# A two-block fp32 model on one core: row broadcasts and square sums from rounded parts, gate activations in pairs, and a reordered delta-rule stage

## The chip, the cores and the metric

The kernel runs on one core of one Trainium2 chip. The metric is the device time of one execution in microseconds, as the median of several executions. All data is fp32 with 512 tokens, and the model's width D is 1024. An activation lies feature-major in SBUF, as 8 tiles of 128 features by 512 tokens.

## What is computed

The reference is a chain of two blocks. Cut to its order and to the parts that the change touches:

```
h = x + 0.5*ffn1(norm(x))
proj = norm(h) @ w_in                       # hybrid mixer ("mixer1")
z, xbc, dt, q, k, v = split(proj)
xs, B, C = split(silu(causal_conv(xbc)))
dt = softplus(dt + dt_bias); a = -exp(a_log)
y = ssd_chunked(xs, dt, a, B, C, d_skip)    # 16 heads of 64
y = norm(y * silu(z))
h = h + concat(y, chunked_rel_attention(q, k, v)) @ w_out
h = norm(h + 0.5*ffn2(norm(h)))
# second block, layer 0: gated delta rule ("mixer2"), 8 heads of 128
q, k, v = split(silu(causal_conv(norm(h) @ w_qkv)))
q, k = l2_norm(q)*128**-.5, l2_norm(k)
beta = sigmoid(b_in); g = -exp(a_log)*softplus(a_in + dt_bias)
G = cumsum(g) in chunks of 64
decay[r,s] = exp(G[r] - G[s]), s <= r
solve (I + strict(beta * k k^T * decay)) [u, w] = [beta v, beta exp(G) k]
o = recurrence over chunks; o = norm(o) * silu(gate)
h = h + o @ w_out; h = h + ffn(norm(h)); h = h + embedding part
# layer 1: stick-breaking attention ("mixer3"), 8 heads of 128
k = norm_per_head(norm(h) @ w_k); q = norm_per_head(norm(h) @ w_q)*128**-.5
```

Then come the attention of mixer3, its FFN and its embedding part.

## The kernel before

Weights stream through one pipeline of 405 units, each 128 partitions by 1024. A unit comes by DMA into one of two `raw` slots. ACT rounds it to `w_hi` (L403, type fp32r), POOL computes `w_lo` = raw - w_hi (L2470), and there are four slots of these. The activations are split in the same way into `x_hi` and `x_lo` (or `mid_hi` and `mid_lo`). PE forms each fp32 product from three fp32r matmuls: hi by hi, lo by hi, hi by lo. A unit for 128 output features is then 24 matmuls of 128 rows by 512 columns. Each engine has its own program, written out by hand in Python functions (`pe_mixer1`, `act_mixer1`, `dve_mixer1` and so on); semaphores join them, and the order on each engine is the order of the code.

**Mixer1.** The cumulative sums of the 16 heads' decays lie in `cs_row`, 16 partitions by 512. For each head x, `broadcast(x)` (L719) spreads row x over 128 partitions into a PSUM bank: an fp32 matmul whose weights are column x of the identity, repeated. DVE subtracts the column form (`exponents`, L1106), ACT takes exponentials (`decays`, L969 and L972), DVE multiplies by C B^T (`weights`, L1119), and PE multiplies by the scaled inputs (`y_pair(m)`, L736 and L741, two heads each). A loop of eight rounds m does this for the heads 2m+2 and 2m+3 and for y_pair(m). Between these, PE works at the 8 units of z (`gate_fill`, L646 to L648), as filler. z of round m+1 goes from PSUM through DVE (`z_out`, L1123) and ACT (`z_silu`, L977); Silu is in another of ACT's function tables than Exp, so ACT loads a table before it and one after it. `gate` (L1131) multiplies y by silu(z), ACT squares it (L992), and `round_at` does the L403 rounding of one weight unit.

**Mixer2.** Units of q, k and v come first; each passes `conv_tile` on DVE (L1731, L1735, L1737 three times) and `conv_silu` on ACT (L1624). Log decays and betas lie in `g_row`, 40 partitions by 512 (rows 0 to 7 and 32 to 39). `decay_broadcast` (L1372) and `beta_broadcast` (L1377) spread one row each, as in mixer1. The heads go in four pairs p. In each, the triangular solve doubles an inverse over levels n: PE L1471, ACT `em` (L1656), PE L1502, DVE L1881 and the transpose L1884. A pair's setup, its four broadcasts too, is done in the levels of the pair before it, and that of pair 0 among the units. `FILLS[p]` names the three filler units that PE does during pair p: units of the output gate (L1324 to L1326, from `x_hi`) and of the output projection (L1335 to L1337, from `mid_hi` and `mid_lo`, which pair p-1 has to have finished). L1452 is the sum of a pair's output norm.

**Mixer3.** Sixteen units give k and q. ACT squares each 128x512 tile, and PE adds over the partitions with a matrix of ones (`square_sum`, L2084, fp32).

## Time and profile before

| | before |
|---|---|
| time, median of 3 runs | 2642.24 us (2640.12 to 2644.57) |
| profiled execution, its own time | 2639.76 us |
| its span | 2638.0 us |
| mean granted TensorE clock | 0.995 |
| busy PE / DVE / ACT / POOL | 98% / 39% / 41% / 40% of the span |
| HBM | 84 GB/s over the span |

The span runs from the first to the last instruction; 1.76 us of the execution's own time lie around it. The profile counts an engine busy while an instruction is in it. Matmuls are pipelined and overlap in the records, so the distance between two starts tells what one costs, not its duration. One fp32 matmul is recorded as two. In a timeline the columns are the start, the time in us, engine, line, operation, output<-inputs and the count; in brackets stands the idle time of the engine just before, with what ended it. A row of windows gives the stretch, its length, the busy time (and instructions) of PE, PEld (weight loads), DVE, ACT and POOL, the granted TensorE clock (1.00 is full speed), the DMA share and GB/s.

### The profile page before, as it was taken

What the parts mean: (1) busy time and instruction counts of PE and PEld (TensorE: products, weight loads), DVE (VectorE), ACT (ScalarE), POOL (GpSimd) and SP (SyncE); (2) the same over time, 40 slices, a digit from 0 to 9 for tenths busy, and PEclk for the clock granted to TensorE, in tenths of its full rate; (3) what the DMA queues carried; (4) which work ended last, traced back from release to release, by engine and by line L of the source; (5) the groups of instructions that cost most, each with busy time, mean ns of one, the idle gap of its engine ahead of it and who ended that gap; (6) DMA issues with size and microseconds to landing.
All of it is one profiled execution on the core that took longest, in us unless ns stands there. A gap on an engine that the chain in (4) does not pass through costs nothing.

```text
span 2638.0 us, 32543 instructions
## 1 busy us (share of the span) xinstructions
PE 2593.3 (98%) x12090; PEld 2100.3 (80%) x12090; DVE 1041.8 (39%) x1477; ACT 1089.7 (41%) x1567; POOL 1060.8 (40%) x466
## 2 busy tenths in 40 slices
PE   9999999999999999999999999999999999999999
PEld 7888887776888888777878878888877777888887
DVE  4212223966522122787456542122372344211224
ACT  5222233678432223565445542223355464222233
POOL 4444443222444444335334344444443222444444
PEclk9999999999999999999999999999999999999999
DMA  4232332111232222222000122322322112222233
GB/s 158 95 101 93 102 125 77 62 56 57 88 103 98 94 96 95 80 80 80 17 25 25 33 96 95 104 89 95 103 89 79 56 48 80 96 96 96 95 103 113
DMA packets 61719, 222.68 MB, mean 84 GB/s; under 512 B 6704, under 2 KB 6832, under 8 KB 61488
## 3 DMA queue, kind: packets, MB, share of 16 engines
q1 hardware_dynamic: 60928, 218.07, 25.0%
q10 hardware_dynamic: 688, 3.15, 0.3%
q8 instruction: 75, 1.23, 0.2%
q14 instruction: 28, 0.23, 0.0%
HBM read 219.10 MB, written 2.10 MB: 84 GB/s over the span
## 4 chain that ended last, share of the span: by engine, by line
PE 91%; DVE 6%; issue 2%; ACT 1%; DMA 0%; SPq 0%; DVEq 0%; ACTq 0%
PE ps L358 13%; PE ps L360 13%; PE ps L359 13%; PE ps L385 6%; PE ps L384 6%; PE ps L383 6%; PE ps L646 2%; PE ps L647 2%; PE ps L648 2%; PE ps L1471 1%; PE ps L1502 1%; PE ps L2187 1%; PE ps L1412 1%; PE ps L1414 1%; PE ps L1413 1%
## 5 line engine op out<-in xcount | busy, mean ns | idle before, releaser
L2470 POOL TENSOR_TENSOR w_lo<-raw,w_hi 128x1024 fp32r<-128x1024 f32 x405 | 981.9, 2426 | 1471.5 <-ACT w_hi L403 1471.5
L403 ACT ACTIVATE w_hi<-raw 128x1024 fp32r<-128x1024 f32 x405 | 424.9, 1050 | 468.2 <-PE ps L385 294.2
L358 PE MATMUL ps<-x_hi,w_hi 128*128 128x512 f32 x1536 | 600.7, 391 | 5.1 <-DVE x_lo L436 5.1
L359 PE MATMUL ps<-x_lo,w_hi 128*128 128x512 f32 x1536 | 597.7, 389 | 0.0
L360 PE MATMUL ps<-x_hi,w_lo 128*128 128x512 f32 x1536 | 597.6, 389 | 0.0
L358 PEld LDWEIGHTS ps<-x_hi,w_hi 128*128 128x128 f32 x1536 | 288.3, 188 | 69.9 <-DVE x_lo L436 6.7
L359 PEld LDWEIGHTS ps<-x_lo,w_hi 128*128 128x128 f32 x1536 | 288.3, 188 | 60.8 <-issue 1.4
L360 PEld LDWEIGHTS ps<-x_hi,w_lo 128*128 128x128 f32 x1536 | 288.3, 188 | 60.0
L383 PE MATMUL ps<-mid_hi,w_hi 128*128 128x512 f32 x736 | 286.3, 389 | 0.0
L384 PE MATMUL ps<-mid_lo,w_hi 128*128 128x512 f32 x736 | 286.3, 389 | 0.0
L385 PE MATMUL ps<-mid_hi,w_lo 128*128 128x512 f32 x736 | 286.3, 389 | 0.0
L530 DVE TENSOR_TENSOR ff_up<-ps,rstd 128x512 f32<-128x512 f32 x88 | 60.8, 691 | 398.5 <-PE ps L360 398.5
L499 ACT ACTIVATE mid_hi<-ff_up 128x512 f32 (+1 forms) x88 | 55.6, 632 | 384.6 <-DVE ff_up L533 384.6
L554 DVE SCALAR_TENSOR_TENSOR h<-ps,h 128x512 f32<-128x512 f32 x64 | 43.8, 690 | 392.3 <-PE ps L385 392.3
L384 PEld LDWEIGHTS ps<-mid_lo,w_hi 128*128 128x128 f32 x736 | 138.2, 188 | 28.8
L383 PEld LDWEIGHTS ps<-mid_hi,w_hi 128*128 128x128 f32 x736 | 138.2, 188 | 28.7
L385 PEld LDWEIGHTS ps<-mid_hi,w_lo 128*128 128x128 f32 x736 | 138.2, 188 | 28.5
L496 ACT ACTIVATE ff_gate<-ff_gate 128x512 f32<-128x512 f32 x88 | 55.6, 632 | 247.8 <-DVE ff_gate L528 247.7
L528 DVE TENSOR_TENSOR ff_gate<-ps,rstd 128x512 f32<-128x512 f32 x88 | 60.8, 691 | 221.2 <-PE ps L360 200.8
L1957 POOL TENSOR_TENSOR ao<-at,const 128x512 f32<-128x512 f32 x48 | 66.5, 1404 | 98.9 <-PE ps L1471 81.2
L535 DVE TENSOR_TENSOR mid_lo<-ff_up,mid_hi 128x512 f32 x88 | 66.9, 761 | 80.1 <-ACT mid_hi L499 80.1
L646 PE MATMUL ps<-x_hi,w_hi 128*128 128x512 f32 x232 | 94.0, 405 | 0.3 <-DVE x_lo L436 0.3
...
## 6 DMA issues: line engine op xcount, KB each, us to landing
...
```

The costliest lines, as they stand in the source:

```text
L358: nc.tensor.matmul(out, hi, x_hi[:, k, :], start=(k == 0), stop=False)
L359: nc.tensor.matmul(out, hi, x_lo[:, k, :], start=False, stop=False)
L360: last = nc.tensor.matmul(out, lo, x_hi[:, k, :], start=False, stop=(k == DK - 1))
L383: nc.tensor.matmul(out, hi, r_hi, start=(k == 0), stop=False)
L384: nc.tensor.matmul(out, hi, r_lo, start=False, stop=False)
L385: last = nc.tensor.matmul(out, lo, r_hi, start=False, stop=(k == tiles - 1))
L403: nc.scalar.activation(w_hi[:, n % W_SLOTS, :], raw[:, n % RAW_SLOTS, :], ACT.Copy).then_inc(s_whi, 1)
L528: nc.vector.tensor_tensor(ff_gate[:, pair, :], ps[:, 4 * g + j % 4, :], rstd[:, :], ALU.mult).then_inc(s_free, 1)
L535: nc.vector.tensor_tensor(tile_at(mid_lo, done), ff_up[:, pair, :], tile_at(mid_hi, done).bitcast(F32), ALU.subtract).then_inc(s_mlo, 1)
L646: nc.tensor.matmul(out, hi, x_hi[:, k, :], start=(k == 0), stop=False)
L1957: nc.gpsimd.tensor_tensor(gw["ao"][j][:, :, :], gw["at"][j][:, :, :], merge, ALU.mult).then_inc(s_gao, 1)
L2470: nc.gpsimd.tensor_tensor(w_lo[:, n % W_SLOTS, :], raw[:, n % RAW_SLOTS, :], w_hi[:, n % W_SLOTS, :].bitcast(F32), ALU.subtract).then_inc( ...
```

## The change

1. Mixer1's 16 broadcasts. A tile `cs_parts` holds the rounded rows in partitions 0 to 15 and the rests in 64 to 79; `sel` is built once, with ones at x and at 64+x. The broadcast becomes one fp32r matmul over 80 rows. DVE builds `cs_parts` with a memset, a copy and a subtraction (semaphore `s_csp`).
2. Mixer2's 16 broadcasts, in the same way over 104 rows (`g_parts`; one ACT copy and two DVE subtractions, `s_gpt`).
3. Mixer1's z. Silu is applied to tiles 0 and 1 before the loop, and then to two tiles at once in rounds 2, 4 and 6. DVE's `z_out` runs two tiles ahead. PE takes 16 instead of 8 of the gate filler's pieces before the loop, so that the loop's last two rounds have output units as filler.
4. Mixer2's last convolution (unit 23 of q, k, v) moves on DVE and ACT from before level 0 of pair 0 to behind the updates of level 0.
5. `FILLS[1]`: gate 3, out(0,0), gate 4 becomes gate 3, gate 4, out(0,0).
6. Mixer3's 16 square sums. DVE squares, ACT copies a rounded part (in place of squaring), DVE subtracts, and PE adds both parts with two fp32r matmuls.

```
-FILLS = ((("gate", 0), ("gate", 1), ("gate", 2)), (("gate", 3), ("out", 0, 0), ("gate", 4)),
+FILLS = ((("gate", 0), ("gate", 1), ("gate", 2)), (("gate", 3), ("gate", 4), ("out", 0, 0)),
...
             def broadcast(x):
                 if x == 0:
+                    pe.wait_ge(s_sel, 1)
+                    pe.wait_ge(s_csp, 3)
...
-                nc.tensor.matmul(ps[:, SPREAD[x % 2], :], ident[0:SSD_HEADS, x:x + 1].to_broadcast([SSD_HEADS, P]), cs_row[:, :],
+                nc.tensor.matmul(ps[:, SPREAD[x % 2], :], sel[0:64 + SSD_HEADS, x:x + 1].to_broadcast([64 + SSD_HEADS, P]), cs_parts[:, :],
...
-            take(gates, 8)
+            take(gates, 16)
...
+                if m < 6:
                     take(gates, 4)
+                else:
+                    out_unit(n_t, 0, 0, (0, 1) if m == 6 else (2, 3))
+                if m < 7:
                     broadcast(2 * m + 3)
-                else:
-                    out_unit(n_t, 0, 0, (0, 1))
                 y_pair(m)
-                if m < 7:
+                if m < 6:
                     take(gates, 4)
             assert next(gates, None) is None
-            out_unit(n_t, 0, 0, (2, 3))
...
             z_silu(0)
+            z_silu(1)
             for m in range(8):
                 if m < 7:
                     decays(2 * m + 2)
+                if m in (2, 4, 6):
+                    z_silu(m)
+                    z_silu(m + 1)
+                if m < 7:
                     decays(2 * m + 3)
...
-                if m < 7:
-                    z_silu(m + 1)
...
+                    if x == 6:
+                        nc.vector.memset(cs_parts[:, :].bitcast(F32), 0.0).then_inc(s_csp, 1)
+                        dve.wait_ge(s_csp, 1)
+                        nc.vector.tensor_copy(cs_parts[0:SSD_HEADS, :], cs_row[:, :]).then_inc(s_csp, 1)
+                        dve.wait_ge(s_csp, 2)
+                        nc.vector.tensor_tensor(cs_parts[64:64 + SSD_HEADS, :], cs_row[:, :], cs_parts[0:SSD_HEADS, :].bitcast(F32), ALU.subtract).then_inc(s_csp, 1)
...
                 if p:
                     pe.wait_ge(s_gqk, x - 1)
-                nc.tensor.matmul(ps[:, SETUP[j], :], ident[0:40, x:x + 1].to_broadcast([40, P]), g_row[:, :], start=True, stop=True).then_inc(s_gbc, 1)
+                elif j == 0:
+                    pe.wait_ge(s_gpt, 3)
+                nc.tensor.matmul(ps[:, SETUP[j], :], sel[0:104, x:x + 1].to_broadcast([104, P]), g_parts[:, :], start=True, stop=True).then_inc(s_gbc, 1)
...
+                if u == 9:
+                    act.wait_ge(s_ga2, 2)
+                    nc.scalar.activation(g_parts[0:40, :], g_row[:, :], ACT.Copy).then_inc(s_gpt, 1)
...
                 if u == 24:
+                    conv_tile(22, 23)
...
+                    if p == 0 and n == 0:
+                        conv_tile(23, 24)
...
-                nc.tensor.matmul(ps[:, 4 + c % 4, :], ones, n_sq3[:, c % 4, :], start=True, stop=True).then_inc(s_nsum, 1)
+                nc.tensor.matmul(ps[:, 4 + c % 4, :], ones_r[:, :], n_hi3[:, c % 4, :], start=True, stop=False)
+                nc.tensor.matmul(ps[:, 4 + c % 4, :], ones_r[:, :], n_lo3[:, c % 3, :], start=False, stop=True).then_inc(s_nsum, 1)
...
-                nc.scalar.activation(n_sq3[:, c % 4, :], src, ACT.Square).then_inc(s_nsq, 1)
+                nc.scalar.activation(n_hi3[:, c % 4, :], n_sq3[:, c % 3, :], ACT.Copy).then_inc(s_nhi, 1)
...
+                if u >= 3:
+                    dve.wait_ge(s_nsum, SUMS + u - 2)
+                dve.wait_ge(s_free, b0 + u + 5)
+                nc.vector.tensor_tensor(n_sq3[:, u % 3, :], dest, dest, ALU.mult).then_inc(s_n32, 1)
+                if u:
+                    square_lo(u - 1)
```

ACT in the middle of mixer1's loop, before. It is one round, from one square (`sq`) to the next; `zs` is z, `decay` the exponentials.
```order
L992 ACTIVATE sq<-zs 128x512
L403 ACTIVATE w_hi<-raw 128x1024
L977 ACT_TABLE_LOAD
L977 ACTIVATE zs<-zs 128x512
L969 ACT_TABLE_LOAD
L969 ACTIVATE decay<-ps,bias_c 128x128 x6
L972 ACTIVATE decay<-decay,bias_c 128x128 x4
L969 ACTIVATE decay<-ps,bias_c 128x128 x6
L972 ACTIVATE decay<-decay,bias_c 128x128 x4
L992 ACTIVATE sq<-zs 128x512
```

The same engine after, from the square of round 1 to that of round 2:
```order
L1009 ACTIVATE sq<-zs 128x512
L409 ACTIVATE w_hi<-raw 128x1024
L981 ACTIVATE decay<-ps,bias_c 128x128 x6
L984 ACTIVATE decay<-decay,bias_c 128x128 x4
L989 ACT_TABLE_LOAD
L989 ACTIVATE zs<-zs 128x512 x2
L981 ACT_TABLE_LOAD
L981 ACTIVATE decay<-ps,bias_c 128x128 x6
L984 ACTIVATE decay<-decay,bias_c 128x128 x4
L1009 ACTIVATE sq<-zs 128x512
```

The gate's activation with its table load and the load back to Exp stood in each round, ahead of both groups of exponentials. Now two tiles stand behind one load, between the two groups of round 2, and round 1 has no load. Over the program ACT's table loads go from 106 to 99.

DVE around level 0 of mixer2's first pair, before: `tm<-tt` is the transpose of the first inverse, `cv` the last convolution, L1881 the update of level 0.
```order
L1770 STREAM_TRANSPOSE tm_117<-tt_115 128x512
L1785 TENSOR_TENSOR g_exp<-g_exp,cols_97 128x32
L1731 TENSOR_TENSOR ps<-ps,rstd 128x512
L1735 TENSOR_SCALAR cv_102<-ps,vec 128x512
L1737 SCALAR_TENSOR_TENSOR cv_102<-ps,vec,cv_102 128x511
L1737 SCALAR_TENSOR_TENSOR cv_102<-ps,vec,cv_102 128x510
L1737 SCALAR_TENSOR_TENSOR cv_102<-ps,vec,cv_102 128x509
L1881 TENSOR_TENSOR tt_114<-tt_114,ps 128x512
L1884 STREAM_TRANSPOSE tm_116<-tt_114 128x512
L1881 TENSOR_TENSOR tt_115<-tt_115,ps 128x512
L1884 STREAM_TRANSPOSE tm_117<-tt_115 128x512
L1865 TENSOR_TENSOR qkt_122<-ps,dm_126 128x512
```

After:
```order
L1805 STREAM_TRANSPOSE tm_120<-tt_118 128x512
L1821 TENSOR_TENSOR g_exp<-g_exp,cols_100 128x32
L1921 TENSOR_TENSOR tt_117<-tt_117,ps 128x512
L1924 STREAM_TRANSPOSE tm_119<-tt_117 128x512
L1921 TENSOR_TENSOR tt_118<-tt_118,ps 128x512
L1924 STREAM_TRANSPOSE tm_120<-tt_118 128x512
L1766 TENSOR_TENSOR ps<-ps,rstd 128x512
L1770 TENSOR_SCALAR cv_105<-ps,vec 128x512
L1772 SCALAR_TENSOR_TENSOR cv_105<-ps,vec,cv_105 128x511
L1772 SCALAR_TENSOR_TENSOR cv_105<-ps,vec,cv_105 128x510
L1772 SCALAR_TENSOR_TENSOR cv_105<-ps,vec,cv_105 128x509
L1905 TENSOR_TENSOR qkt_125<-ps,dm_129 128x512
```

The convolution's five operations went from ahead of the level's updates to behind them.

PE in pair 1 of mixer2, before: `g_row,const` are the decay broadcasts, `tt,em` and `tm,ao` the products of the levels, `mid_hi` and `mid_lo` belong to the unit out(0,0).
```order
L1372 MATMUL ps<-g_row,const 128x512 x2
L1502 MATMUL ps<-tt_114,em_110 128x128 x4
L1502 MATMUL ps<-tt_115,em_111 128x128 x4
L1335 MATMUL ps<-mid_hi,w_hi 128x512
L1336 MATMUL ps<-mid_lo,w_hi 128x512
L1337 MATMUL ps<-mid_hi,w_lo 128x512
L1335 MATMUL ps<-mid_hi,w_hi 128x512
L1336 MATMUL ps<-mid_lo,w_hi 128x512
L1337 MATMUL ps<-mid_hi,w_lo 128x512
L1471 MATMUL ps<-tm_116,ao_108 128x128 x4
L1471 MATMUL ps<-tm_117,ao_109 128x128 x4
```

After, at the same rows of the order:
```order
L1396 MATMUL ps<-g_parts,sel 128x512 x2
L1526 MATMUL ps<-tt_117,em_113 128x128 x4
L1526 MATMUL ps<-tt_118,em_114 128x128 x4
L1346 MATMUL ps<-x_hi,w_hi 128x512
L1347 MATMUL ps<-x_lo,w_hi 128x512
L1348 MATMUL ps<-x_hi,w_lo 128x512
L1346 MATMUL ps<-x_hi,w_hi 128x512
L1347 MATMUL ps<-x_lo,w_hi 128x512
L1348 MATMUL ps<-x_hi,w_lo 128x512
L1495 MATMUL ps<-tm_119,ao_111 128x128 x4
L1495 MATMUL ps<-tm_120,ao_112 128x128 x4
```

The broadcasts read `g_parts` and `sel`, and the filler here is now a unit of the gate; out(0,0) comes later in the pair.

## Rows read from the trace of the kernel before

**Rows 1.** The page: busy time, and the chain that ended last, by engine.
```profile
PE 2593.3 (98%) x12090; PEld 2100.3 (80%) x12090; DVE 1041.8 (39%) x1477; ACT 1089.7 (41%) x1567; POOL 1060.8 (40%) x466
...
PE 91%; DVE 6%; issue 2%; ACT 1%; DMA 0%; SPq 0%; DVEq 0%; ACTq 0%
```

**Rows 2.** Timeline of PE: two broadcasts of mixer2's head, then 16 rounded matmuls.
```profile
1206.36 0.39 PE L1414 MATMUL ps<-x_hi,w_lo 128*128 128x512 f32 x1
1206.68 1.98 PE L1372 MATMUL ps<-g_row,const 40*128 40x512 f32 x4
...
1208.92 0.40 PE L1413 MATMUL ps<-x_lo,w_hi 128*128 128x512 f32 x1
...
1222.67 0.40 PE L1412 MATMUL ps<-x_hi,w_hi 128*128 128x512 f32 x1
...
1226.08 0.39 PE L1412 MATMUL ps<-x_hi,w_hi 128*128 128x512 f32 x1
```

**Rows 3.** Timeline of PE at one broadcast in mixer1's loop.
```profile
579.08 1.12 PE L719 MATMUL ps<-cs_row,const 16*128 16x512 f32 x2
580.13 0.44 PE L736 MATMUL ps<-decay,xdt 128*64 128x128 f32 x4
```

**Rows 4.** Timeline of PE in mixer3: two square sums, 24 rounded matmuls between them.
```profile
2012.11 1.02 PE L2084 MATMUL ps<-n_sq,const 128*128 128x512 f32 x2
...
2018.46 0.59 PE L2084 MATMUL ps<-n_sq,const 128*128 128x512 f32 x1
```

**Rows 5.** One round of mixer1's loop: busy times; timelines of DVE and ACT.
```profile
573.33:584.08 10.75, 10.75 (x62) 7.07 (x61) 7.10 (x10) 10.40 (x25) 2.38 (x1) 1.00 0.15 49
...
576.24 0.69 DVE L1106 TENSOR_TENSOR decay<-ps,cols 128x512 f32<-128x512 f32 x1 [0.80 <-PE ps L719]
...
577.51 1.48 DVE L1119 TENSOR_TENSOR decay<-decay,cb 128x1280 f32<-128x1280 f32 x1
...
574.93 1.28 ACT L977 ACT_TABLE_LOAD   x1
```

**Rows 6.** Mixer1's last round: timelines of DVE, POOL and PE.
```profile
639.88 3.36 DVE L1119 TENSOR_TENSOR decay<-decay,cb 128x1280 f32<-128x1280 f32 x1
...
639.50 2.40 POOL L2470 TENSOR_TENSOR w_lo<-raw,w_hi 128x1024 fp32r<-128x1024 f32 x1 [8.38 <-ACT w_hi L403]
...
643.30 0.44 PE L736 MATMUL ps<-decay,xdt 128*64 128x128 f32 x4 [1.34 <-DVE decay L1119]
```

**Rows 7.** Windows: the number before the DMA share is the granted clock.
```profile
643.00:647.00 4.00, 3.70 (x34) 2.79 (x35) 1.47 (x3) 0.00 (x0) 0.00 (x0) 1.00 0.33 122
1246.00:1250.00 4.00, 4.00 (x18) 3.90 (x19) 1.72 (x3) 1.24 (x2) 2.36 (x1) 0.50 0.00 0
```

**Rows 8.** Timelines of DVE and PE in mixer2's head and level 0.
```profile
1227.64 0.70 DVE L1731 TENSOR_TENSOR ps<-ps,rstd 128x512 f32<-128x512 f32 x1 [1.95 <-PE ps L1414]
...
1240.83 0.69 DVE L1731 TENSOR_TENSOR ps<-ps,rstd 128x512 f32<-128x512 f32 x1
...
1242.34 2.32 DVE L1737 SCALAR_TENSOR_TENSOR cv<-ps,vec,cv 128x511 f32<-128x511 f32 x3
...
1245.86 0.58 PE L1502 MATMUL ps<-tt,em 128*128 128x128 f32 x1 [4.11 <-ACT em L1656]
```

**Rows 9.** Timeline of PE in mixer2's pairs: norm sums (L1452) and waits.
```profile
1306.75 0.70 PE L1452 MATMUL ps<-o_sq,const 128*128 128x512 f32 x1 [0.95 <-ACT o_sq L1697]
...
1337.12 0.76 PE L1335 MATMUL ps<-mid_hi,w_hi 128*128 128x512 f32 x1 [3.83 <-DVE mid_lo L1859]
...
1377.79 0.70 PE L1452 MATMUL ps<-o_sq,const 128*128 128x512 f32 x1 [0.95 <-ACT o_sq L1697]
...
1406.29 0.35 PE L1471 MATMUL ps<-tm,ao 128*128 128x128 f32 x1 [0.55 <-DVE tm L1884]
...
1443.58 0.70 PE L1452 MATMUL ps<-o_sq,const 128*128 128x512 f32 x1 [0.95 <-ACT o_sq L1697]
...
1472.08 0.55 PE L1471 MATMUL ps<-tm,ao 128*128 128x128 f32 x1 [2.60 <-DVE tm L1884]
```

More of the change, by code:

```diff
@@ L261, in build @@
         total_c = place("total_c", M + 50 * KB + 1184, [P, NB, SSD_HEADS])
+        cs_parts = place("cs_parts", M + 14 * KB, [64 + SSD_HEADS, T], F32R)
         y_tmp = place("y_tmp", M + 16 * KB, [P, 2, T])
@@ L267, in build @@
         v2 = place("v2", M + 32 * KB, [P, 8, T])
-        g_row = place("g_row", M + 48 * KB, [40, T])
+        g_row = place("g_row", MID_HI + 38 * KB, [40, T])
+        g_parts = place("g_parts", M + 48 * KB, [104, T], F32R)
         cols2 = place("cols2", M + 50 * KB, [P, NB, 40])
@@ L592, in build @@
         s_csb = sem("cumsum_broadcast")
+        s_sel = sem("row_selectors_ready")
+        s_csp = sem("cumsum_parts_ready")
+        s_gpt = sem("gdn_row_parts_ready")
         s_dec = sem("decay_ready")
@@ L1376, in beta_broadcast @@
                 pe.wait_ge(s_gem, x + 1)
-                nc.tensor.matmul(ps[:, SETUP[j], :], ident[0:40, 32 + x:33 + x].to_broadcast([40, P]), g_row[:, :], start=True, stop=True).then_inc(s_gbb, 1)
+                nc.tensor.matmul(ps[:, SETUP[j], :], sel[0:104, 32 + x:33 + x].to_broadcast([104, P]), g_parts[:, :], start=True, stop=True).then_inc(s_gbb, 1)
             def products_of_k(p, j):
@@ L1596, in norms, with conv_silu @@
                 nc.scalar.activation(n_rs[:, :, :], n_rs[:, :, :], ACT.Exp, scale=-0.5).then_inc(s_nrs, 1)
+            def conv_silu(c):
+                act.wait_ge(s_conv, 12 + c + 1)
+                dest = qk2[:, c, :] if c < 16 else v2[:, c - 16, :]
+                nc.scalar.activation(dest, cv2[:, c % 4, :], ACT.Silu).then_inc(s_convact, 1)
             for u in range(N_QKV):
@@ L1716, in dve_mixer2 @@
             ch.step(nc.vector.memset(g_row[:, :], 0.0))
+            nc.vector.memset(g_parts[:, :].bitcast(F32), 0.0)
             dve.wait_ge(s_rfin, 1)
@@ L1812, in dve_mixer2 @@
                     nc.vector.tensor_copy(cols2[:, :, :], ps[:, 7, 0:256].rearrange("p (a c) -> p a c", a=NB)[:, :, 0:40]).then_inc(s_gcol, 1)
+                if u == 10:
+                    dve.wait_ge(s_gpt, 1)
+                    for at in (0, 32):
+                        nc.vector.tensor_tensor(g_parts[64 + at:72 + at, :], g_row[at:at + 8, :], g_parts[at:at + 8, :].bitcast(F32), ALU.subtract).then_inc(s_gpt, 1)
                 if u == 22:
```

38 lines of the change are left out of this document (26 added, 12 removed).

## The prediction

> **What bounds the kernel now.** I read the page first: PE is busy 98% of the span and holds 91% of the chain that ended last, DVE 6%; DVE, ACT and POOL are busy 39 to 41% [rows 1]. So the kernel is bound by PE nearly everywhere. Time comes from cheaper PE work, or from one of its few waits; work added to the other engines is free as long as it makes no new wait on PE. Next the PE timeline gives the price of each kind of matmul, the distance between two starts. Last I read where another engine ends PE's wait: ACT or DVE once in mixer1's last round [rows 6], at level 0 of mixer2 [rows 8], and in its pairs [rows 9]. The windows tell what such a wait costs beyond itself: after one of 4.11 us the granted clock is 0.50, which is 1.2 GHz, for the four microseconds behind it; after one of 1.34 us it stays 1.00, which is 2.4 GHz [rows 7].
>
> **The price of a broadcast.** Fifteen rounded matmuls take 1226.08 - 1222.67 = 3.41 us, so 0.227 each. Two fp32 broadcasts and two rounded matmuls take 1208.92 - 1206.36 = 2.56 us, so 2.56 - 0.454 = 2.106 for the two, 1.05 each [rows 2]. Mixer1's are the same: 1.05 from the broadcast's start to the next matmul's [rows 3]. The square sums, fp32 too, but over all 128 rows, cost less: two starts with 24 rounded matmuls between them are 6.35 us apart, less 24 x 0.227 = 5.45, leaves 0.90 [rows 4]. The new broadcast is one rounded 128x512 matmul over 80 or 104 rows. Lower bound 0.227; upper bound, if a matmul of fewer than 128 rows keeps what a K=16 or 40 one has over the full one, 1.05 - 0.90 = 0.15 more. I take 0.227, since it is nearly a full one and of the type of its neighbours. The matmul behind a broadcast also starts about 0.1 late in every second case (1206.36 to 1206.68 is 0.32, not 0.227 [rows 2]). Saving: 1.05 - 0.23 + 0.05 = 0.87 each.
>
> The Trainium skill (TensorEngine Tiling (Array Packing), Key Properties) says that a change of tiling mode drains TensorE, and gives row tiling to contractions of up to 64 rows; 80 and 104 are beyond that, so by it no drain would remain, and the difference of 1.05 to 0.90 agrees with it. By the page the sum would be the one below; if the drain stayed it would be rival A.
>
> **Mixer1's loop.** A round lasts 10.75 us, PE is busy for all of it and ACT for 10.40 [rows 5]. PE's work becomes 10.75 - 2 x 0.82 - 0.1 = 9.0. ACT could not follow at 10.40; the paired silus take away 2 x 1.28 of table loads in rounds without z [rows 5], leaving 7.8, and in a round with two z it has 10.40 + 0.69 = 11.1 (a second silu, taken as long as DVE's pass over 128x512), which the rounds around it make up for. DVE's chain is next: a broadcast lands (0.39), exponents and scaled inputs take 577.51 - 576.24 = 1.27, L1119 takes 1.48 [rows 5], plus 0.1 of hand-over: 3.25 from one broadcast to the next, against PE's 0.227 + 12 x 0.227 = 2.95. So PE waits 0.3 in a plain round. L1119 is worse where POOL works: the same operation took 3.36 beside a w_lo that started 0.38 us before it, so 1.88 more [rows 6]. In the shorter round it meets a w_lo oftener. I followed the instructions of all eight rounds forward by these durations: extra waits of 1.4, 0.7, 1.5 and 0.7 in rounds 1, 2, 4 and 6, 0.3 in each of the other three, and 3.1 in the last instead of 1.34 [rows 6], since round 6's pair (two table loads and two silus, 2 x 1.28 + 2 x 0.69 = 3.9) makes its decays late. Gain: 16 x 0.87 = 13.9, less 4.3, 0.9 and 1.8, makes **7** (5 if the waits are doubled in the rounds with POOL, 9 if POOL is never in the way). Building `cs_parts` I cost at nothing: it lies in DVE's part among units, where PE has its own 5.45 us of work per unit and DVE one conv; without that cover it costs three operations, 1.5.
>
> The Trainium skill (SBUF — State Buffer, Terms) says that VectorE and GpSimd share a port pair, held for the full instruction, and that "the loser fully blocks". The 3.36 beside 1.48 agrees. It speaks against this change, which puts more two-input work on DVE; by it alone the loop would lose what I subtract above, and mixer3 could become rival B.
>
> **Mixer2's head.** Its four broadcasts save PE 3.5, but DVE sets the pace here: it waited for PE only 1.95 [rows 8], so 1.95 counts. Then level 0. PE waited 4.11 for ACT's `em` [rows 8], which stood behind the silu of the last convolution; that convolution ran on DVE from 1240.83 to 1244.66, 3.83 us [rows 8]. Moved behind the level, it takes this wait away. But the transposes of v in level 1 still need it, and PE has only about 1 us of work beside it: a new wait of 2.9 (0 to 3.8). The clock of 0.50 in the four microseconds after [rows 7] costs 2.0; the new wait is between 1.34, without a fall, and 4.11, with one, so I count half, 1.0. Sum 1.95 + 4.11 - 2.9 + 1.0 = **4.2** (2 to 7).
>
> **Mixer2's pairs.** During pair 0: four broadcasts, 3.5, of which I count **3.0**, as some wait for ACT. During pair 1: the filler out(0,0) made PE wait 3.83 for `mid_lo`. The period from norm sum to norm sum is 1377.79 - 1306.75 = 71.04; the next, with the same kinds of work and no such wait, is 1443.58 - 1377.79 = 65.79 [rows 9]. The difference, **5.25**, is the wait and the slow clock behind it, and the reorder takes it: gate 4 needs only `x_hi` and its weights, and out(0,0) comes some 10 us later, when `mid_lo` has been written. Broadcasts in pairs 1 and 2: eight, but the four decay broadcasts come just before a wait of 0.55 for DVE's transpose at 1406.29 [rows 9], which grows by what they save; the four beta broadcasts count, 4 x 0.87 less a little: **3.3**. Pair 3's waits (2.60 at 1472.08 [rows 9]) are untouched. New waits of 2 to 3 us in all this can lower the clock once: **-1.1**, half of a 2 us drop. Mixer2 together: 4.2 + 3.0 + 5.25 + 3.3 - 1.1 = 14.65. Extra ACT and DVE work for `g_parts` is three small operations in units 9 and 10, where DVE waits for PE.
>
> **Mixer3.** A square sum costs 0.90 and becomes 2 x 0.227: 0.45 x 16 = **7.1**. A unit shortens from 6.35 to 5.9. DVE now has three 128x512 operations for each (scaling, square, rest), 3 x 0.69 = 2.1 by the nearest row [rows 5], plus a w_lo's 2.40 [rows 6] if it is in the way: 4.5 of 5.9. Covered, so 0 here; if two w_lo's block it each time, rival B.
>
> **Sum.** 7 + 14.65 + 7.1 = 28.75. From the profiled execution, 2639.76, this leads to 2611.0. The median of before lies 2.48 above that execution: 2642.24 - 28.75 = **2613.5**.
>
> **Rivals.** A: the short matmuls keep their surcharge. 32 x 0.15 = 4.8, a little of it hidden where DVE sets the pace: 4, so 2617.5. For it: both fp32 broadcasts with few rows show the surcharge [rows 2 to 4]. Against: 80 and 104 rows are most of the array. Chance 0.10. B: DVE bounds mixer3. Each unit needs DVE for 2.1 + 2 x 2.40 = 6.9 instead of PE's 5.9, 16 us over sixteen units: 2629.5. For it: every added square and rest can meet a w_lo. Against: one w_lo falls to one unit in the steady state, and 4.5 fits. Chance 0.10. C, slower than before: PE's clock falls to 1.2 GHz after the new waits of mixer1's loop and mixer2 and stays down. To take back the gain of 28.75 and 5.3 more, the margin below, needs 34 us lost, that is 68 us of PE time at half clock, about a whole loop of mixer1; the time would be 2648 or more. It decides from eight rounds' worth of low clock. Against: the clock was 1.00 after a wait of 1.34 [rows 7], and the loop's waits are mostly smaller. Chance 0.03. D: the change does nothing to the time, since PE's shorter work turns into equal waits in all three stages: 2642, chance 0.04. It needs DVE chains within 1 us of PE everywhere, against DVE's 7.10 of 10.75 in the busiest loop [rows 5]. The forecast itself: 0.73.
>
> **Range.** The forecast's terms, with their ends: mixer1 5 to 9, mixer2 9 to 18, mixer3 5 to 7.1; ends that don't all fall together give 2604 to 2622, which holds nearly all of the forecast's 0.73 and rival A, 0.8 in all. B, C and D lie outside. A difference of 0.2%, about 5.3 us, is what a measurement of this kernel can tell from no change. Faster by more: forecast, A and B, with a little less for a combination, 0.93; within it: 0.04; slower: 0.03.
>
> **What would show it.** In the profile after: a broadcast on PE takes 0.23 to the next start (0.38 would be A). Mixer1's rounds are 9.3 to 10.5, with a wait for L1119's successor of some 3 us in the last. Level 0 of pair 0 has no wait for `em`; one of about 3 us stands before the v transposes. The wait for `mid_lo` in pair 1 is gone, and the period is near 64. In mixer3 the units are 5.9 apart and PE waits for nothing; a wait for the squares or for a bank (B) would make the prediction too low. Wrong, too, if the mean clock falls below 0.99.

## The result and the profile after

The changed kernel takes 2622.19 us, the median of four runs (2620.69 to 2628.02), against 2641.18 (2638.73 to 2644.57) before: a ratio of 0.9934, with a 95% interval of 0.9921 to 0.9946. Measured again beside other kernels it took 2620.37 against 2643.18, ratio 0.9915 (0.9899 to 0.9930). So it is 19 to 23 us faster. I had forecast 28.75 us less. The direction was right; the size was not, and the first median lies 0.2 us above the range; the second, 2620.37, lies inside it.

The profiled execution is the slowest of the four (2628.02, span 2626.2), so what it shows must be split into what the change did and what that execution had. The page, its rows for [rows 1]:
```profile
PE 2566.5 (98%) x12058; PEld 2097.4 (80%) x12058; DVE 1088.5 (41%) x1517; ACT 1080.9 (41%) x1561; POOL 1066.2 (41%) x466
...
PE 87%; DVE 9%; issue 2%; ACT 1%; DMA 0%; SPq 0%; DVEq 0%; ACTq 0%
```

PE is busy for 26.8 us less. The span is only 11.8 us shorter, and DVE went from 6% of the chain to 9%: the work taken off PE partly became waits for DVE.

To see where the time went I set the start of each w_lo on POOL (405 in every kernel, one for each weight unit), and of L1452 (now L1476), against the same one before. The differences by stage, in us, negative where a stage became shorter (the experiments are explained below; the last row is a second profile of the kernel before). "pair3+" is pair 3 and the rest of mixer2, "attn3" all from mixer3's attention on; nothing was changed in either:

```
                start  mixer1  head+pair0  pair1  pair2  pair3+  mixer3  attn3
forecast          0     -7.0      -7.2     -6.9   -1.6     0      -7.1     0
changed         +2.2    +0.3      -5.8     -3.7   -0.4   -2.5     -3.7   +2.0
e1_again        +2.3    -6.0      -5.4     -4.1   -1.6     0      -3.6   +0.3
e2_no_mixer1    +3.9     0        -7.6     -3.7   -0.5   -2.5     -3.7   +1.7
e3_no_sums3     +2.3    -7.7      -6.1     -4.2   -1.6     0       0     +0.3
e4_full_rows    -0.2    -7.8      -6.2     -4.1   -1.5   +0.1     -3.6   +0.3
e5_no_fills     +0.5    -3.8      -6.3     -2.4   -0.3   -1.1     -3.7   +1.9
e6_no_conv      +2.6    -6.1      -3.9     -2.6   -0.4     0      -3.8    0
e7_no_bcast2    +2.6    -7.8      -3.6     -3.7    0     -0.9     -3.7    0
e8_no_z         -0.3    -5.1      -6.2     -3.7   -0.4   -0.1     -3.8    0
e9_ahead_first  +1.8    -6.1      -6.0     -4.2   -1.6     0      -6.6   +0.2
e10_w_first     -0.4    -8.2      -5.0     -4.1   -1.6     0      -3.7   +0.2
e11_both        +3.9    -8.1      -7.3     -3.7   -0.4     0      -6.6   +1.9
e12_before      +2.0     0        +0.2     +0.1    0       0       0     -0.1
```

Of the forecast, 1.1 for slow clock stands in no column. "Start" is the lag at the fortieth unit, ahead of all that was changed. The last row says that a lag of this size needs no change: the same w_lo starts at 216.18 in the kernel before, at 218.34 in the changed one and at 218.13 in the second profile of the kernel before.

The two columns in which nothing was changed show mostly what the clock does. In pair 3 of the kernel before the granted clock is 0.74 and 0.83 over 1470 to 1478 us, and 0.61 over 1520 to 1524, behind waits of 2.60 and 2.78; in the profile of the changed kernel it is 1.00 at both places behind waits of 2.59 and 2.78, which makes the 2.5 us. It lost 2.0 again in mixer3's attention (last section). So a gain of 2.5 and a loss of 2.0 in this profile belong to no part of the change.

Mixer1 in the changed kernel. PE's timeline at two broadcasts (for [rows 3]) and at the longer waits of the rounds:
```profile
569.73 0.48 PE L730 MATMUL ps<-cs_parts,sel 80*128 80x512 f32 x1
570.05 0.40 PE L655 MATMUL ps<-x_hi,w_hi 128*128 128x512 f32 x1
572.57 0.39 PE L657 MATMUL ps<-x_hi,w_lo 128*128 128x512 f32 x1
573.05 0.49 PE L730 MATMUL ps<-cs_parts,sel 80*128 80x512 f32 x1
573.48 0.44 PE L747 MATMUL ps<-decay,xdt 128*64 128x128 f32 x4
...
583.47 0.49 PE L730 MATMUL ps<-cs_parts,sel 80*128 80x512 f32 x1 [1.22 <-DVE decay L1134]
...
624.56 0.79 PE L730 MATMUL ps<-cs_parts,sel 80*128 80x512 f32 x1 [2.32 <-DVE decay L1134]
```

The windows of the same kernel behind the last of these waits, with the granted clock ahead of the DMA share:
```profile
624.00:632.00 8.00, 7.44 (x36) 5.13 (x37) 4.63 (x6) 3.44 (x12) 0.00 (x0) 0.57 0.21 66
```

A broadcast is one matmul now; the next one starts 0.32 or 0.43 us after it, instead of 1.05. In rounds 1, 2, 4 and 5 there are waits of 1.22, 0.65 (at 593.30), 1.24 (at 613.04) and 2.32 us before the second broadcast; I had 1.4, 0.7 and 1.5 in the first three, and 0.7 in round 6 instead of one in round 5. Around the last the granted clock is 0.57 over eight microseconds, so it was at 1.2 GHz for most of them and at 2.4 for the rest. It fell a second time, to 0.79 over 640 to 648, at the last wait of the loop (3.13 at 645.78). Who holds PE up is seen on DVE:
```profile
610.37 2.61 DVE L1134 TENSOR_TENSOR decay<-decay,cb 128x1280 f32<-128x1280 f32 x1
614.19 1.48 DVE L1134 TENSOR_TENSOR decay<-decay,cb 128x1280 f32<-128x1280 f32 x1
...
620.81 3.69 DVE L1134 TENSOR_TENSOR decay<-decay,cb 128x1280 f32<-128x1280 f32 x1
```

and on POOL in the same stretch:
```profile
609.23 2.40 POOL L2527 TENSOR_TENSOR w_lo<-raw,w_hi 128x1024 fp32r<-128x1024 f32 x1 [4.43 <-ACT w_hi L409]
620.77 2.38 POOL L2527 TENSOR_TENSOR w_lo<-raw,w_hi 128x1024 fp32r<-128x1024 f32 x1 [9.14 <-ACT w_hi L409]
```

L1134, the L1119 of before, takes 1.48 where POOL is idle (614.19), 2.61 when a w_lo began 1.14 before it, and 3.69 when one began 0.04 before it. That is the blocking of [rows 6], in a place where PE waits for it. Waiting for the rest of the w_lo's 2.40 and then taking 1.48 would be 2.74 and 3.84, within 0.15 of both. The Trainium skill (SBUF — State Buffer, Terms) calls the port pair of VectorE and GpSimd exclusive for a full instruction; the three durations agree.

Mixer2 in the changed kernel, PE's timeline at the new wait for the v transposes (L1506), the waits of pair 1, and the norm sums that answer to [rows 9]:
```profile
1251.09 0.44 PE L1506 MATMUL ps<-const,v 128*128 128x128 f32 x2 [2.57 <-DVEq L1778]
...
1303.39 0.70 PE L1476 MATMUL ps<-o_sq,const 128*128 128x512 f32 x1 [0.95 <-ACT o_sq L1731]
...
1331.89 0.35 PE L1495 MATMUL ps<-tm,ao 128*128 128x128 f32 x1 [2.20 <-DVE tm L1924]
...
1361.07 0.50 PE L1357 MATMUL ps<-mid_hi,w_hi 128*128 128x512 f32 x1 [1.86 <-DVE gate L1874]
...
1370.73 0.70 PE L1476 MATMUL ps<-o_sq,const 128*128 128x512 f32 x1 [0.95 <-ACT o_sq L1731]
```

The wait of 4.11 for `em` is gone, and one of 2.57 stands at the v transposes, as forecast (2.9). The wait of 3.83 for `mid_lo` is gone too. But two others stand in pair 1: 2.20 for DVE's transpose, and 1.86 for DVE's `gate`, at the unit out(0,0) in its new place. DVE starts that `gate` only at 1360.36, straight after an inverse and its transpose (L1803 at 1358.13, L1805 at 1359.72).

Mixer3 in the changed kernel: PE's timeline from one square sum to the next:
```profile
1975.98 0.39 PE L2128 MATMUL ps<-n_hi,ones_r 128*128 128x512 f32 x1
...
1981.88 0.39 PE L2128 MATMUL ps<-n_hi,ones_r 128*128 128x512 f32 x1
...
1988.59 0.50 PE L2128 MATMUL ps<-n_hi,ones_r 128*128 128x512 f32 x1 [0.66 <-DVE n_lo L2387]
```

DVE's timeline there, with the square (L2396) and the rest (L2387):
```profile
1976.98 0.69 DVE L2396 TENSOR_TENSOR n_sq<-k 128x512 f32<-128x512 f32 x1
...
1982.87 2.85 DVE L2396 TENSOR_TENSOR n_sq<-k 128x512 f32<-128x512 f32 x1
1985.65 2.88 DVE L2387 TENSOR_TENSOR n_lo<-n_sq,n_hi 128x512 fp32r<-128x512 f32 x1
```

and POOL's:
```profile
1982.77 5.21 POOL L2527 TENSOR_TENSOR w_lo<-raw,w_hi 128x1024 fp32r<-128x1024 f32 x2 [8.73 <-ACT w_hi L409]
```

A plain unit takes 1981.88 - 1975.98 = 5.90, as forecast; the next takes 6.71, with a wait of 0.66 for the rest `n_lo`. There POOL has two w_lo's back to back, 5.21 us, and DVE's square and rest take 2.85 and 2.88 instead of 0.69.

### The profile page after: what moved, and what is told of

It is laid out like the page before. It is cut to its first block, busy times and chain, and to the rows that moved or that the text cites. A ratio compares the mean times of both kernels' runs of the same rounds, so it can differ in the third digit from the quotient of the medians.

```text
span 2626.2 us, 32527 instructions
## 1 busy us (share of the span) xinstructions
PE 2566.5 (98%) x12058; PEld 2097.4 (80%) x12058; DVE 1088.5 (41%) x1517; ACT 1080.9 (41%) x1561; POOL 1066.2 (41%) x466
## 4 chain that ended last, share of the span: by engine, by line
PE 87%; DVE 9%; issue 2%; ACT 1%; DMA 0%; SPq 0%; DVEq 0%; ACTq 0%
PE ps L364 13%; PE ps L366 13%; PE ps L365 13%; PE ps L390 6%; PE ps L391 6%; PE ps L389 6%; PE ps L655 2%; PE ps L656 2%; PE ps L657 2%; PE ps L2232 1%; PE ps L1495 1%; PE ps L1526 1%; DVE cv L1772 1%; PE ps L1436 1%; PE ps L1437 1%
## 5 line engine op out<-in xcount | busy, mean ns | idle before, releaser
L541 DVE TENSOR_TENSOR mid_lo<-ff_up,mid_hi 128x512 f32 x88 | 66.9, 760 | 80.1 <-ACT mid_hi L505 80.1
```

The costliest lines, as they stand in the source:

```text
L541: nc.vector.tensor_tensor(tile_at(mid_lo, done), ff_up[:, pair, :], tile_at(mid_hi, done).bitcast(F32), ALU.subtract).then_inc(s_mlo, 1)
```

## The experiments

All are compared with the kernel before on the same chip. The median of one and the same kernel moves by about 2 us from one measurement to the next (2641.18 to 2643.18 before, 2622.19 and 2620.37 after), so the parts are read from the traces, in the table above, and the medians only confirm them. Each stage of a variant is one profiled execution.

**e1_again** is the changed kernel once more.

> The changed kernel once more, unchanged. Theory 1 (chance falls of the clock): in the trace of the changed kernel the granted clock fell in mixer1's loop (0.57 over 624 to 632 us, 0.79 over 640 to 648), which cost about 6 us there, and again behind a wait of 2.35 us in mixer3's attention, 2 us, and the first units ran 2.2 us late; a second profile will miss at least one of these, and mixer1 will then show a gain near 6 us over before instead of a loss of 0.3. Theory 2 (the loop's new waits always bring the clock down): the second profile shows the same falls at the same places, and mixer1 gains nothing again. Time: about 2621 by the first, 2622 to 2628 by the second.

Measured: 2620.37 us, ratio 0.9915 (0.9899 to 0.9930). Mixer1 gains 6.0 in this profile and lost 0.3 in the first. The windows over the stretch in which the clock had fallen:
```profile
624.00:632.00 8.00, 7.94 (x51) 5.89 (x47) 7.64 (x9) 6.44 (x21) 3.09 (x2) 1.00 0.18 66
```

PE's timeline at the last wait of the loop:
```profile
640.74 0.44 PE L747 MATMUL ps<-decay,xdt 128*64 128x128 f32 x4 [2.04 <-DVE decay L1134]
```

Here round 5 has no such wait (0.11) and round 6 has one of 0.82, and the clock stayed at 1.00 over 624 to 632. It fell only at the last wait, to 0.79 over 640 to 648. DVE's and POOL's timelines show what made the difference in round 5, to be held against 620.81 and 620.77 above:
```profile
620.99 1.48 DVE L1134 TENSOR_TENSOR decay<-decay,cb 128x1280 f32<-128x1280 f32 x1
```

and
```profile
621.01 3.69 POOL L2527 TENSOR_TENSOR w_lo<-raw,w_hi 128x1024 fp32r<-128x1024 f32 x1 [9.19 <-ACT w_hi L409]
```

In the first profile w_lo began 0.04 us before L1134, and L1134 took 3.69; here it began 0.02 us after it, L1134 took 1.48, and it was w_lo that took 3.69 instead of 2.40. Of the two, the one that started first was not held up. Theory 1 holds for mixer1: a start 0.06 us earlier or later decided which of the two waited, and so whether PE waited 2.32 or 0.11. The fall in mixer3's attention is missing here too; the start was late again.

**e2_no_mixer1** undoes the whole of mixer1's part:

```
-                nc.tensor.matmul(ps[:, SPREAD[x % 2], :], sel[0:64 + SSD_HEADS, x:x + 1].to_broadcast([64 + SSD_HEADS, P]), cs_parts[:, :],
+                nc.tensor.matmul(ps[:, SPREAD[x % 2], :], ident[0:SSD_HEADS, x:x + 1].to_broadcast([SSD_HEADS, P]), cs_row[:, :],
...
-            take(gates, 16)
+            take(gates, 8)
```

(and the orders of `z_out`, `z_silu` and the filler as before.)

> The changed kernel with mixer1 as before (fp32 broadcasts, one silu a round, the old filler split); all else changed. If mixer1's part gains what I forecast less the waits (theory 1), this is 5 to 7 us slower than the changed kernel; if the new waits and the clock take it all (theory 2), it is within 1 us of it or faster, and its profile has no fall of the clock in mixer1.

Measured: 2625.33, 5.0 us over e1_again, measured beside it. Mixer1's part is worth 5 us on the median. Its profile has no fall of the clock in mixer1.

**e3_no_sums3** undoes mixer3's sums:

```
-                nc.tensor.matmul(ps[:, 4 + c % 4, :], ones_r[:, :], n_hi3[:, c % 4, :], start=True, stop=False)
-                nc.tensor.matmul(ps[:, 4 + c % 4, :], ones_r[:, :], n_lo3[:, c % 3, :], start=False, stop=True).then_inc(s_nsum, 1)
+                nc.tensor.matmul(ps[:, 4 + c % 4, :], ones, n_sq3[:, c % 4, :], start=True, stop=True).then_inc(s_nsum, 1)
```

> The changed kernel with mixer3's square sums as before (fp32 ones matmul, ACT squares). Prediction's term: 7.1 us slower than the changed kernel. Rival reading of the changed kernel's trace: three units of the sixteen wait 0.66 us for DVE's rest and start late, because two w_lo's of POOL run back to back and hold two DVE operations for 2.8 us each, and the first units gain nothing; then it is 3.5 to 4 us slower only.

Measured: 2622.85, 2.5 us over e1_again; in the traces mixer3 gains 0 here and 3.6 there. The rival reading is right: half of my 7.1.

**e4_full_rows** makes both kinds of broadcast 128 rows long:

```
-sel[0:64 + SSD_HEADS, x:x + 1].to_broadcast([64 + SSD_HEADS, P])
+sel[:, x:x + 1].to_broadcast([P, P])
```

> The changed kernel with both kinds of broadcast over all 128 rows (the added rows are zero in the moving data). If matmuls over 80 and 104 rows still pay for being short (rival A: in the changed trace the start after a mixer1 broadcast is 0.32 to 0.43 us later and the start before it 0.48, instead of 0.23), these distances fall to 0.23 and the time falls by 2 to 5 us. If that distance comes from what stands beside the broadcast (fp32 and 64-column matmuls), nothing changes: within 1 us.

Measured: 2619.01, within the runs of e1_again (2618.80 to 2623.24). PE's timeline, to be held against 569.73 to 573.48 above:
```profile
567.31 0.48 PE L730 MATMUL ps<-cs_parts,sel 128*128 128x512 f32 x1
567.62 0.40 PE L655 MATMUL ps<-x_hi,w_hi 128*128 128x512 f32 x1
570.16 0.39 PE L657 MATMUL ps<-x_hi,w_lo 128*128 128x512 f32 x1
570.63 0.50 PE L730 MATMUL ps<-cs_parts,sel 128*128 128x512 f32 x1
571.06 0.33 PE L747 MATMUL ps<-decay,xdt 128*64 128x128 f32 x2
```

The distances are 0.31 and 0.43, as with 80 rows. Rival A is refuted: the short matmul pays nothing. What is left over 0.227 comes from the neighbours: in the head of mixer2, between rounded matmuls of 512 columns, two broadcasts over 104 rows take 0.47, 0.235 each (PE's timeline in e1_again):
```profile
1203.20 0.63 PE L1396 MATMUL ps<-g_parts,sel 104*128 104x512 f32 x2
1203.67 0.40 PE L1436 MATMUL ps<-x_hi,w_hi 128*128 128x512 f32 x1
```

The rule of the Trainium skill that I quoted (TensorEngine Tiling (Array Packing), Key Properties, and for the 64 rows The Problem) leads to the same, no drain for 80 or 104 rows. Whether a drain is what made the fp32 broadcasts over 16 and 40 rows dearer than the square sums over 128, no run shows.

**e5_no_fills** sets `FILLS[1]` back.

```
-(("gate", 3), ("gate", 4), ("out", 0, 0)),
+(("gate", 3), ("out", 0, 0), ("gate", 4)),
```

> The changed kernel with FILLS[1] as before (gate 3, out(0,0), gate 4). Prediction's term: 5.25 us for the reorder. In the changed kernel's traces pair 1 lasts 66.9 us instead of the 64.1 that I forecast, with a wait of 2.21 for DVE's transpose and one of 1.87 for DVE's gate that weren't there; by that reading the reorder brings about 3 us, so this is 3 us slower than the changed kernel, and its pair 1 lasts 69 to 70 us with the wait for mid_lo of 3.8. By the prediction it would be 5 us slower.

Measured: 2624.33, ratio 0.9931 (0.9917 to 0.9944). PE's timeline in pair 1, at the first matmul of out(0,0):
```profile
1327.52 0.77 PE L1357 MATMUL ps<-mid_hi,w_hi 128*128 128x512 f32 x1 [5.48 <-DVE mid_lo L1899]
```

From norm sum to norm sum (1297.13 to 1365.75) the pair lasts 68.62, 1.7 us longer than in e1_again and 1.3 longer than in the first profile. The windows over pair 1, first the kernel before, then this one:
```profile
1306.75:1377.79 71.04, 65.31 (x417) 55.17 (x417) 39.46 (x60) 33.36 (x71) 26.31 (x17) 0.95 0.08 23
1297.13:1365.75 68.62, 61.09 (x412) 53.73 (x412) 39.45 (x60) 33.33 (x71) 26.34 (x17) 0.95 0.07 24
```

The length less PE's busy time is PE's idle time: 5.73 before, 7.53 here. The wait for `mid_lo` is 5.48 instead of 3.83: what the two decay broadcasts ahead of it save is added to it. The two beta broadcasts come behind it, and what they save stays. So the broadcasts alone bring 2.4. I had expected a pair of 69 to 70 us, 3 us longer, with a wait of 3.8.

**e6_no_conv** puts the last convolution ahead of level 0 again.

```
-                if 1 <= u < 23:
+                if u:
                     conv_tile(u - 1, u)
...
-                    if p == 0 and n == 0:
-                        conv_tile(23, 24)
```

> The changed kernel with mixer2's last convolution ahead of level 0 again. Prediction: 4.11 of wait and half of 2 us of slow clock come back, the 2.9 us wait for the v transposes (2.45 to 2.57 in the traces) goes: 2.2 us slower than the changed kernel, 3.6 if the clock falls each time behind the wait of 4.11. If the move only trades one wait for another, within 0.7 us.

Measured: 2625.75, ratio 0.9944 (0.9931 to 0.9958). PE's timeline shows the wait again:
```profile
1241.45 3.78 PE L1526 MATMUL ps<-tt,em 128*128 128x128 f32 x16 [4.11 <-ACT em L1683]
```

Sixteen matmuls take 3.78 behind it, as slow as before. The head and pair 0 gain 3.9, against 5.0 to 7.6 (6.2 on average) in the ten profiles in which this part is as in the changed kernel: the move is worth about 2, and I had 2.2. Pair 1, in which this kernel is as the changed one, gains only 2.6 here; the granted clock is 0.95 over it, as before, and 0.97 in e1_again.

**e7_no_bcast2** undoes mixer2's broadcasts, and the building of `g_parts`.

```
-                elif j == 0:
-                    pe.wait_ge(s_gpt, 3)
-                nc.tensor.matmul(ps[:, SETUP[j], :], sel[0:104, x:x + 1].to_broadcast([104, P]), g_parts[:, :], start=True, stop=True).then_inc(s_gbc, 1)
+                nc.tensor.matmul(ps[:, SETUP[j], :], ident[0:40, x:x + 1].to_broadcast([40, P]), g_row[:, :], start=True, stop=True).then_inc(s_gbc, 1)
```

> The changed kernel with mixer2's 16 broadcasts in fp32 over 40 rows again. Prediction: 1.95 (head) + 3.0 (pair 0) + 3.3 (pairs 1 and 2) = 8.2 us slower. If DVE's chain sets more of the pace than I took (the new waits of 2.21 for the transposes in pairs 1 and 2 are that), 4 to 6 us slower.

Measured: 2622.64, ratio 0.9934 (0.9920 to 0.9948). That is 0.5 to 2.3 us over the changed kernel, less than either expectation. By the traces, the head and pair 0 gain 3.6 instead of about 6.2, pair 1 3.7 instead of 4.1, pair 2 nothing instead of 1.6 at best. The sixteen broadcasts are worth 2.6 + 0.4 + 1.6 = 4.6, where I had 8.2. The wait for DVE's transpose in pair 1 tells a part of why:
```profile
1326.41 0.46 PE L1492 MATMUL ps<-tm,ao 128*128 128x128 f32 x2 [0.55 <-DVE tm L1913]
```

It is 0.55 with the old broadcasts and 2.2 with the new: what the two decay broadcasts save goes into it, as I had taken. In the head, all kernels with the new broadcasts have a wait of 0.83 to 2.05 us for DVE at L1408, which is not there in this one. The other part is the clock. The windows over pair 1, here and in e1_again:
```profile
1297.92:1365.22 67.30, 63.18 (x417) 53.18 (x417) 40.55 (x60) 33.23 (x71) 27.63 (x17) 1.00 0.07 25
1297.68:1364.61 66.93, 61.16 (x413) 54.19 (x413) 40.48 (x60) 33.27 (x71) 27.31 (x17) 0.97 0.07 25
```

With the old broadcasts the granted clock is 1.00 over the pair, and over the whole of 1100 to 1298 us; with the new ones it is 0.97 and 0.97. Over all five executions of this kernel the mean granted clock is 0.996 to 0.999, over the eight of the changed kernel 0.994 to 0.996. So a part of what the cheaper broadcasts save is given back at a lower clock; which wait decides this was not tried.

These rows split pair 1. The reorder alone (this kernel against the one before, with the same matmuls) takes 1.6 off PE's idle time (4.12 for 5.73), since `gate` (1.86) and the transposes (0.55) hold PE up in place of `mid_lo` (3.83), and 2.1 off its busy time, with the clock at 1.00 for 0.95: 3.7. The broadcasts alone bring 2.4 (e5). Both together bring 3.7 to 4.2, or 2.6 with the clock at 0.95 (e6): PE's idle time is then 5.77, as before, and its busy time 4.15 less.

**e8_no_z** sets the z order of mixer1 back and keeps the rounded broadcasts.

```
-            z_silu(1)
...
-                if m in (2, 4, 6):
-                    z_silu(m)
-                    z_silu(m + 1)
...
+                if m < 7:
+                    z_silu(m + 1)
```

> The changed kernel with one silu a round in mixer1 again (the rounded broadcasts stay). ACT then has 10.4 us of work in each round against PE's 9.0 to 9.3, so rounds last 10.4 to 10.7 and PE waits over 1 us in each: by the prediction this takes back nearly all of mixer1's 7, 5 to 7 us slower than the changed kernel. If the table loads were not what bounds the shortened round, within 2 us of it.

Measured: 2622.09, ratio 0.9933 (0.9920 to 0.9947). Mixer1 gains 5.1. PE's timeline has a wait in each round; this is the third:
```profile
587.06 0.50 PE L730 MATMUL ps<-cs_parts,sel 80*128 80x512 f32 x1 [1.41 <-DVE decay L1130]
```

The windows over the same wait:
```profile
584.00:592.00 8.00, 6.59 (x47) 4.68 (x46) 6.38 (x6) 7.92 (x23) 1.66 (x1) 1.00 0.21 68
```

Seven waits of 0.9 to 1.4 and a round of 10.6 us: ACT is the bound, as expected. But the stage gains 5.1 and not next to nothing: 2.2 up to w_lo 96 (the two broadcasts ahead of the loop and its first rounds), 0.6 in the middle up to w_lo 100, and 2.3 at its end, where PE has no last wait. So the pairing is worth 2.7 (7.8 less 5.1) in an execution in which the clock stays up, 1 where it falls at the last wait alone (e1, e6, e9), and it costs 1.3 to 5.4 where it falls in mid-loop (e5, the first profile): 0.5 on average. The median says the same, 2622.09 against 2620.37 to 2622.19 for the changed kernel.

**e9_ahead_first** swaps one order on ACT in mixer3.

```
-                if u in (6, 10, 14):
-                    norms(u // 4 - 1)
                 if u:
                     act_ahead(act, n0, 0, u)
+                if u in (6, 10, 14):
+                    norms(u // 4 - 1)
+                if u:
                     square(u - 1)
```

> The changed kernel with one order swapped on ACT in mixer3: in units 6, 10 and 14 the rounding of the next weights stands ahead of the norm's Ln and Exp (5.1 us) instead of behind them. Theory (two w_lo's back to back on POOL, 5.2 us, hold DVE's square and rest for 2.8 us each, so PE waits 0.66 and starts late, 0.83 us in each of three units): the three waits go, and mixer3 as a whole gains 2.5 us more than in the changed kernel, 6.1 instead of 3.6 against before. If PE's waits there come from ACT's copies being late and not from POOL, the waits stay or grow.

Measured: 2617.11, ratio 0.9907 (0.9890 to 0.9924). POOL's timeline in this kernel:
```profile
1979.21 2.40 POOL L2528 TENSOR_TENSOR w_lo<-raw,w_hi 128x1024 fp32r<-128x1024 f32 x1 [5.35 <-ACT w_hi L409]
1983.10 2.55 POOL L2528 TENSOR_TENSOR w_lo<-raw,w_hi 128x1024 fp32r<-128x1024 f32 x1 [1.49 <-ACT w_hi L409]
```

PE's timeline at three square sums:
```profile
1975.81 0.39 PE L2128 MATMUL ps<-n_hi,ones_r 128*128 128x512 f32 x1
...
1981.70 0.39 PE L2128 MATMUL ps<-n_hi,ones_r 128*128 128x512 f32 x1
...
1987.59 0.39 PE L2128 MATMUL ps<-n_hi,ones_r 128*128 128x512 f32 x1
```

The two w_lo's are apart, the units are 5.89 and 5.89, the three waits are gone, and mixer3 gains 6.6 of the 7.1. The theory holds. Single operations of DVE still take up to 2.9 us beside a w_lo here, without a wait on PE.

**e10_w_first** swaps one order on ACT in mixer1's loop.

```
+                round_at(13 + m)
                 act.wait_ge(s_yg, m + 1)
                 if m >= 2:
                     act.wait_ge(s_ysum, m - 1)
                 nc.scalar.activation(sq[:, m % 2, :], zs[:, m, :], ACT.Square).then_inc(s_ysq, 1)
-                round_at(13 + m)
```

> The changed kernel with one order swapped on ACT in mixer1's loop: the rounding of the next weights ahead of the square of the gated output. POOL's w_lo then starts about 1.1 us earlier in a round. Theory (the loop's waits of 1.2 to 2.3 are DVE's L1134 held up by a w_lo that began just before it): in rounds 1, 3 and 5 it is out of the way, the waits of 0.65 to 1.25 shrink to 0.3 or nothing and the loop ends 2 to 3 us earlier, without falls of the clock. If the waits come from DVE's own chain, they stay as they are.

Measured: 2617.69, ratio 0.9909 (0.9892 to 0.9926). PE's timeline has three waits in the loop:
```profile
580.08 0.49 PE L730 MATMUL ps<-cs_parts,sel 80*128 80x512 f32 x1 [0.34 <-DVE decay L1134]
...
608.39 0.50 PE L730 MATMUL ps<-cs_parts,sel 80*128 80x512 f32 x1 [0.55 <-DVE decay L1134]
...
635.89 0.33 PE L747 MATMUL ps<-decay,xdt 128*64 128x128 f32 x2 [3.14 <-DVE decay L1134]
```

Mixer1 gains 8.2 here and 8.1 in e11, against a loss of 0.3 to a gain of 7.8 with the old order. The waits in mid-loop were POOL's: they sum to 0.9 instead of 3.9 (e1_again). The last, 3.11 to 3.14 us, became longer: I had forecast 3.1 for it, and it was 2.0 in the profiles with short waits in mid-loop. The clock did not stay up, as I had expected; it fell at this last wait, to 0.80 over 632 to 640. Against the profiles with the old order and a fall at that place alone (6.0 to 6.1), the swap is worth 2.1.

**e11_both** has both swaps.

> Both swaps together. By the two theories 4 to 5 us faster than the changed kernel: about 2616 us, ratio to before near 0.990. If either theory fails, its part is missing.

Measured: 2615.42, ratio 0.9898 (0.9882 to 0.9915), the fastest of all; 1.7 to 2.3 us under e9 and e10, which were measured beside it. Both parts are there in its trace, 8.1 in mixer1 and 6.6 in mixer3.

**e12_before** is the kernel before again, one execution.

> The kernel before once more, for a second profile. If the 2 to 4 us that the changed kernels' first weights come late (and -0.2 in one of them) are chance of the input's load and not of the change, this profile shows an offset of that size too; and the granted clock behind the waits of 2.60 at 1472 us and 2.37 at 2177 us will not be the same as in the first profile.

Measured: 2641.93. The start is 2.0 us late here too: the first expectation is borne out. The second is not: behind the wait of 2.60 the clock fell again (0.57 over 1474 to 1478), and behind the one of 2.37 it was 1.00 again.

In the head of mixer2, PE lost 1.5 us at about 1080 us in this profile, with the clock at 0.57 over 1078 to 1082, and had made it up by the start of the pairs. Most changed kernels lose 1.2 to 1.5 us some 25 us later, from another cause: the DMA of one weight unit took 4.8 to 5.1 us from issue to landing, against 3.5 to 4.2 in both profiles of the kernel before and in e1, e2, e10 and e11. They had not made it up by the start of the pairs, likely since the DVE idle time of [rows 8] was already used up there; that was not tried by itself.

## Why the prediction was right in its direction and wrong in its size

Averages over the profiles in which a stage was as in the changed kernel give: mixer1 5.6 (8 profiles), head and pair 0 6.2 (10), pair 1 3.8 (10), pair 2 0.9 (11), mixer3 3.7 (9). The sum is 20.2, inside the measured 19 to 22.8. By the prediction's steps:

- **The price of a broadcast** was nearly right. It is 0.235 between rounded matmuls (I took 0.227), but 0.32 or 0.43 to the next start in mixer1's loop, around the 0.38 that I had named as the sign of rival A; e4 shows that the neighbours cause it and not the number of rows. In mixer1, with PE idle for 6.3 us in the loop instead of 1.35 and a gain of 7.8 (e4), the sixteen saved 12.8, 0.80 each instead of 0.87.
- **Mixer1's loop**, 7: the mechanism held, the mid-loop waits of e1 within 0.3 us of those worked out. The size, 7.8 in executions without a fall of the clock, held in part by luck: the broadcasts saved 1.1 less than I had, and the waits cost 5.0 instead of 7.0, as the last was 2.0 instead of 3.1 and the plain rounds had 0.1 instead of 0.3. What I had not priced here was the clock. At the last wait, of 2.0, it fell in three of six profiles (e1, e6 and e9, not e3, e4 and e7; 1.7 us each), and around a mid-loop wait of 2.3 in the changed kernel and in e5. That takes the mean to 5.6. I had put this under rival C as all or nothing; it came as single falls.
- **Mixer2's head and pair 0**, 4.2 + 3.0: the convolution's move was right (2 against 2.2). The broadcasts brought 2.6 instead of 4.95: PE waits for DVE at L1408, and the clock falls, which it does not in e7.
- **Mixer2's pairs** is one failed step: "The difference, 5.25, is the wait and the slow clock behind it, and the reorder takes it". It took 3.7 alone (e7), and 1.3 to 1.7 on top of the broadcasts (e5). I took the wait of 3.83 as gone and asked nothing of what stood behind it: the transposes hold PE up for 0.55, and out(0,0) in its new place waits 1.86 for the bank that DVE's `gate` must free, and DVE has the state's update and an inverse to do first. So 1.6 of the 3.83 came off. Of the slow clock, the reorder alone took all, 2.1; with the new broadcasts it fell again in this pair. The beta broadcasts' term was sound: in pair 2 it gives 1.5 to 1.6 in five profiles, and 0.3 to 0.5 where the clock fell there. Pair 1 was short by 3.1 of 6.9 in all, pair 2 by 0.7 of 1.65.
- **Mixer3** is the other failed step, and the largest: "Covered, so 0 here". I counted one w_lo in a unit and put two under rival B as a case of all sixteen units. The truth is three units of sixteen: ACT's norm batch delays two weight roundings, which then come together. 3.7 instead of 7.1; e9 takes the cause away and gets 6.6. What is missing there is in the first units, which shorten by 0.3 to 0.4 instead of 0.45.
- **The clock allowance**, 1.1, was set for one new fall in mixer2. New falls came there, in pair 2 in six of the eleven profiles with the new broadcasts; they are in the stages' measured gains already, so the allowance offsets a part of the terms' errors: these (1.4 + 1.0 + 3.1 + 0.7 + 3.4) are 9.6, the sum's is only 8.5.
- **The range** does not follow from its terms. The ends 5 to 9, 9 to 18 and 5 to 7.1 add up to 19 to 34.1, so 2608 to 2623; the 2604 lies beyond all of them, and 2622 leaves out the low end, where the first median is. And its mixer3 part began at 5, though rival B's rows were in hand.

Of the signs named ahead, the waits for `em` and `mid_lo` went and the mean clock stayed above 0.99 (0.994), as forecast; the period of pair 1 is 67.3 or 66.9 and not near 64, and PE has three waits in mixer3 where I had none.

What is left open: why a weight unit comes some 1.4 us late in mixer2's head in most executions and not in all (the profiles show that its DMA took longer to land, not why), and why the clock falls in mixer2 with the new broadcasts and not in e7.
